# The last head of a gated-linear layer in a streaming encoder: its jobs over 21 slots for 18, its silu and splits at other places

## The reference

```python
b = jnp.cumsum(logf, axis=1)
inter = jnp.einsum('blhk,bhkv->blhv', qf * jnp.exp(b), s0)
decay = jnp.exp(jnp.where(causal, b[:, :, None] - b[:, None, :], -jnp.inf))
attn = jnp.einsum('blhk,bmhk,blmhk->bhlm', qf, kf, decay)
intra = jnp.einsum('bhlm,bmhv->blhv', attn, vf)
s_new = jnp.exp(b_last)[..., None] * s0 + jnp.einsum('blhk,blhv->bhkv', k_dec, vf)
...
o = o * lax.rsqrt(jnp.mean(o * o, axis=-1, keepdims=True) + EPS)
o = (o * g_onorm * jax.nn.silu(r)) @ w_out
```

## Time and profile before

| | us |
|---|---|
| median of 3 runs | 2671.1 (2668.15 to 2671.66) |
| the profiled execution | 2670.47 |
| its span, first to last instruction | 2668.7 |
| TensorE busy | 2531.0 |
| VectorE busy | 967.9 |
| ScalarE busy | 822.0 |
| GpSimd busy | 445.0 |
| mean granted TensorE clock, 1 is 2.4 GHz | 0.971 |

### The profile page before, as it was taken

The page is one execution under the profiler, slowest core; times in us unless marked ns, Lnnn a source line. Parts: engine busy times, 40 slices in busy tenths (PEclk is TensorE's granted clock), DMA queues, the critical chain, the costliest instruction groups (busy, mean ns, idle before and its releaser), DMA issues.

```text
span 2668.7 us, 41573 instructions
## 1 busy us (share of the span) xinstructions
PE 2531.0 (95%) x17454; PEld 2388.1 (89%) x17454; DVE 967.9 (36%) x1913; ACT 822.0 (31%) x1618; POOL 445.0 (17%) x186
## 2 busy tenths in 40 slices
PE   6999999898999999999998999889899999999997
PEld 5778878698999999999997977688899999999996
DVE  6354454416422222222228344425522222222227
ACT  4445444335311211120224355535411211211221
POOL 1101110111112211212211010112112212211210
PEclk9999999899999999999999999999999999999998
DMA  3101010013211111111113200103311111111113
GB/s 106 41 9 47 25 39 26 29 48 114 80 40 48 44 42 47 39 47 39 57 42 119 80 25 18 37 25 98 95 48 40 47 39 47 42 44 47 39 60 123
DMA packets 63088, 139.05 MB, mean 52 GB/s; under 512 B 8688, under 2 KB 39920, under 8 KB 62960
## 3 DMA queue, kind: packets, MB, share of 16 engines
q1 hardware_dynamic: 33984, 103.60, 12.0%
q10 hardware_dynamic: 28976, 33.64, 4.1%
HBM read 117.81 MB, written 19.40 MB: 51 GB/s over the span
## 4 chain that ended last, share of the span: by engine, by line
PE 77%; DVE 5%; issue 2%; ACT 2%; ACTq 0%; DMA 0%; DVEq 0%; SPq 0%
PE banks L201 51%; PE banks L181 19%; PE banks L1769 1%; DVE h_lo L548 1%; DVE norm_acc_x L477 1%; DVE norm_acc L463 1%; DVE y L524 1%; PE banks L1269 1%; PE banks L1288 1%; PE banks L323 0%; PE banks L1256 0%; PE banks L1296 0%; PE banks L1922 0%; PE banks L1925 0%; ACT y L1422 0%
## 5 line engine op out<-in xcount | busy, mean ns | idle before, releaser
L158 POOL TENSOR_TENSOR w_lo<-w_raw,w_hi 128x1024 fp32r<-128x1024 f32 x180 | 443.4, 2467 | 2151.3 <-ACT w_hi L151 2151.3
L181 PE MATMUL banks<-h_hi,w_hi 128*128 128x384 f32 (+1 forms) x1224 | 437.9, 358 | 8.1 <-POOL w_lo L158 5.3
L181 PE MATMUL banks<-h_lo,w_hi 128*128 128x384 f32 (+1 forms) x1224 | 415.9, 340 | 0.0
L181 PE MATMUL banks<-h_hi,w_lo 128*128 128x384 f32 (+1 forms) x1224 | 414.5, 339 | 0.0
L151 ACT CAST w_hi<-w_raw 128x1024 fp32r<-128x1024 f32 x180 | 187.0, 1047 | 468.0 <-DMA w_raw<-in_units 467.1
L201 PE MATMUL banks<-h_hi,w_hi 128*128 128x384 f32 (+1 forms) x1368 | 301.7, 329 | 0.0
L201 PE MATMUL banks<-h_hi,w_lo 128*128 128x384 f32 (+1 forms) x1368 | 301.3, 328 | 0.0
L201 PE MATMUL banks<-h_lo,w_hi 128*128 128x384 f32 (+1 forms) x1368 | 301.3, 328 | 0.0
L201 PE MATMUL banks<-mlp_a_hi,w_hi 128*128 128x384 f32 (+1 forms) x1344 | 296.6, 329 | 1.5 <-issue 1.3
L201 PE MATMUL banks<-mlp_a_lo,w_hi 128*128 128x384 f32 (+1 forms) x1344 | 295.1, 327 | 0.0
L201 PE MATMUL banks<-mlp_a_hi,w_lo 128*128 128x384 f32 (+1 forms) x1344 | 295.0, 327 | 0.0
(11 more groups left out here) (191 smaller groups left out, 3108.3 us busy)
## 6 DMA issues: line engine op xcount, KB each, us to landing
w_raw<-in_units SPq DMA_DIRECT2D x180, 512.0 KB, 3.5
x_scratch<-y ACTq DMA_DIRECT2D x48, 192.0 KB, 2.5
norm_x<-x_scratch ACTq DMA_DIRECT2D x48, 192.0 KB, 3.3
x_scratch<-y ACTq DMA_DIRECT2D x24, 160.0 KB, 1.8
norm_x<-x_scratch ACTq DMA_DIRECT2D x24, 160.0 KB, 3.1
y<-in_x SPq DMA_DIRECT2D x16, 192.0 KB, 4.7
norm_x<-in_x ACTq DMA_DIRECT2D x16, 192.0 KB, 3.5
out_y<-y SPq DMA_DIRECT2D x16, 192.0 KB, 2.7
```

The costliest lines, as they stand in the source:

```text
L158: c.nc.gpsimd.tensor_tensor(c.w_lo[:, s], c.w_raw[:, s], c.w_hi[:, s].bitcast(F32), ALU.subtract).then_inc(self.ready, 1)
L181: mm = chip.nc.tensor.matmul(out, w, x, start=(first and n == 0), stop=(last and n == 2))
```

## The change

Only `Gla` is touched. The probability rows of the windowed attention, kept without gaps between the two chunks of a pair (`ROW = WIN + 1`, `prob_keys`), are the same in both kernels.

- Head 3's jobs are spread over 21 slots, so over pairs 0 to 6, for 18 (pairs 0 to 5).
- Its weight casts move to later slots: unit 5 of the head from slot 6 to 8, 6 from 11 to 13, 7 from 13 to 15, 8 from 16 to 18, and 9 from 21 to 24.
- No end part stands in the loop any more; all four follow behind it.
- On ScalarE `silu(3)` and `early_high(0)` move from the end of pair 6 to the middle of pair 7, behind the copy of the turned keys and before the copy of the output. `early_high(1)` moves from the end of pair 7 to the same place in pair 8.
- On VectorE `early_low(0)` moves from the end of pair 6 to the end of pair 7, `early_low(1)` from the end of pair 7 to behind the inverse root of the outputs, and `early_low(2)` from there to behind the gating of block 1 and the first `low_parts`.
- At the start of head 0 the cast of unit 4 moves ahead of the first exponentials, and that of unit 5 ahead of the copy of the last v tile.

```diff
--- before.py
+++ after.py
@@ -1591,11 +1591,10 @@
     SCAN = 9 * CHUNK
     EARLY = 2 * (GH - 1)
     LEAD = 3 * KT * BMAX
-    STEPS = (PARTS * NPAIR, PARTS * NPAIR, PARTS * NPAIR, 18)
+    STEPS = (PARTS * NPAIR, PARTS * NPAIR, PARTS * NPAIR, 21)
     GATE_AT = (1, 3, 3)
     HIGHS = ({2: 6, 4: 7, 10: 8, 15: 9}, {4: 4, 6: 5, 10: 6, 13: 7, 16: 8, 19: 9}, {4: 4, 6: 5, 10: 6, 13: 7, 16: 8, 19: 9},
-             {4: 4, 6: 5, 11: 6, 13: 7, 16: 8, 21: 9})
-    FILL_AT = (23, 25)
+             {4: 4, 8: 5, 13: 6, 15: 7, 18: 8, 24: 9})
 
     def __init__(self, chip, name, before, after, ins):
         self.chip, self.before, self.after, self.ins = chip, before, after, ins
@@ -1844,8 +1843,6 @@
         def fill(h, slot):
             for job, k in self.plan[h][slot]:
                 job_step(job, k)
-            if h == GH - 1 and slot in self.FILL_AT:
-                end_early(self.FILL_AT.index(slot))
 
         def end_early(m):
 
@@ -1959,7 +1956,7 @@
                 output(h, p)
                 fill(h, self.PARTS * p + 2)
 
-        for m in range(len(self.FILL_AT), JOB_BANKS):
+        for m in range(JOB_BANKS):
             end_early(m)
         for i in range(2 * NB):
             if i == 0:
@@ -2189,12 +2186,12 @@
         take_start(2, 1)
         take_start(2, 2)
         chunk_decays(0)
+        ws.high(act, 4)
         level_exp(0)
         copy_value(7)
         level_exp(1)
-        ws.high(act, 4)
+        ws.high(act, 5)
         copy_value(8)
-        ws.high(act, 5)
         take_jobs(0, -1)
 
         for h in range(GH):
@@ -2211,6 +2208,11 @@
                 else:
                     take_jobs(h, slot)
                     level_exp(g + 2)
+                if h == GH - 1 and p == 7:
+                    silu(h)
+                    early_high(0)
+                if h == GH - 1 and p == 8:
+                    early_high(1)
                 if slot in self.HIGHS[h]:
                     ws.high(act, self.unit(h, self.HIGHS[h][slot]))
                 if h < GH - 1 and p == self.GATE_AT[h] + 1:
@@ -2233,11 +2235,6 @@
                     load_gain(h)
                 if h < GH - 2 and p == 6:
                     load_gate(h + 2)
-                if h == GH - 1 and p == 6:
-                    silu(h)
-                    early_high(0)
-                if h == GH - 1 and p == 7:
-                    early_high(1)
         output_root(GH)
         for j in range(NB):
             scale_outputs(GH, j)
@@ -2448,16 +2445,18 @@
                     gate_flat(h + 1)
                 if h < GH - 1 and p == self.GATE_AT[h] + 1:
                     gate_sums(h + 1)
-                if h == GH - 1 and p in (6, 7):
-                    early_low(p - 6)
+                if h == GH - 1 and p == 7:
+                    early_low(0)
         output_variance(GH)
         output_inverse(GH)
-        early_low(2)
+        early_low(1)
         for j in range(NB):
             gated(GH - 1, 2 * j)
             gated(GH - 1, 2 * j + 1)
             if j:
                 low_parts(j - 1)
+            if j == 1:
+                early_low(2)
         low_parts(NB - 1)
         self.vector_end_wave(dve)
```

## The result

The changed kernel takes 2649.61 us (median of 4 runs, 2646.81 to 2655.24) against 2671.38 (4 runs, 2668.15 to 2675.23): a ratio of 0.9921, 95% interval 0.9899 to 0.9942. The profiled execution took 2646.81 us, 23.7 less than that of before (2670.47).

A forecast was written before the change was run, and what follows sets the result against it. TensorE, busy 95% of the span, was taken as the bound. Start -0.3 us and head 3 with its tail -13.2 us sum to -13.5 us against the profiled execution's 2670.5 us: 2657.0 us, range 2651.5 to 2663.

The forecast's parts named there:

- Head 3: The last head of the gated-linear stage, through its tail: the stage ends at 537.7 us against 550.9, -13.2 us.
- The stall of pair 2: Head 3, pair 2: gating behind the update delays the state, a new TensorE stall of 2.2 us before the output's second half.
- rival C: Head 3, pairs 3 to 6: TensorE stays at 1.2 GHz, about 6.2 us per pair, 2682 us with all four; chance 0.04.
- Pair 7: Head 3, pair 7: ScalarE becomes the end, 6.95 us from scores to scores against 18.2.
- End parts: Four end parts behind head 3's loop: 72 matmuls, 12.7 us at full clock, 14.5 us with 1.8 for low clock.
- the late load: Weight load for the cast at slot 24: its 4.5 us wait is covered by the end parts and costs nothing.
- Rival D: Head 3, pairs 7 and 8 last 8.9 and 4.1 us, held by another round: 2 us more, 2659 us; chance 0.13.
- rival B: Low clock in head 3's pair 2 and end parts worth less, 2654.5 us, or more, 2659 us; chance 0.22.
- part 3: The tail, from head 3's turns to the stage's end, with the third low split moved: 4.2 us against 7.3.
- Part 4: Start of head 0, earlier weight cast: -0.3 us, with VectorE's differences blocked by GpSimd's split.
- rival A: Start of head 0: no lock on VectorE's differences, so the earlier cast gives 2.3 us, 2655.0 us; chance 0.12.
- none of these: Whole kernel: an outcome that neither the forecast nor any listed rival describes; chance 0.03.

The follow-up runs named there:

- gate_late: The changed kernel with VectorE gating turn jobs 4 and 5 of head 3 behind the state update of pair 2: 2644.74 us, 0.9904.
- head_only: The changed kernel with the start of head 0 put back to the old order: 2657.46 us, 0.9940 of the kernel before.
- pad_22: The changed kernel with 22 useless transpositions ahead of the scores of pair 1 of head 0: 2653.31 us, 0.9925 of the kernel before.
- silu_old: The changed kernel with the silu and the splits of blocks 0 and 1 back at the ends of pairs 6 and 7: 2659.53 us, 0.9950.
- tail_old: The changed kernel with VectorE's low split of block 2 back ahead of the gating: 2650.65 us, 0.9916 of the kernel before.
- before_pad24: The kernel before with 24 useless transpositions ahead of the scores of pair 1 of head 0: 2665.0 us against 2670.65, 0.9979.
- after_pad62: The changed kernel with 62 useless transpositions ahead of the scores of pair 1 of head 0: 2658.69 us, 0.9949 of the kernel before.
- copy_first: The changed kernel with the copy of the last v tile ahead of the second cast at the start of head 0: 2653.42 us, 0.9935.
- start_only: The kernel before with only the two weight casts moved at the start of head 0: 2665.27 us against 2672.67, 0.9972.
- slots18: The changed kernel with head 3's jobs over 18 slots again and its casts at the old slots but the last: 2655.21 us, 0.9932.
- after_again: The changed kernel without an edit, run a second time: 2649.57 us, 0.9915 of the kernel before.

## Why the prediction was right in head 3 and wrong in the time

**Head 3: -13.2 forecast, -12.6 measured.** The same code of head 3 lasts 113.5 to 117.0 us in the three traces that have the old one, and 102.6 to 105.2 in the six that have the new one unedited, by how much low clock falls into it: so a gain of some 11 us is sure (the means are 115.5 and 104.1), and that forecast and trace agree to 0.6 us is in part luck. Term by term, forecast and then after:
- First scores to the scores of pair 7: 74.5 us, measured 75.5 (424.40 to 499.87). The stall of pair 2 was forecast at 2.2 us and measures 1.87, and gate_late shows its cause. The pair itself was put at 11.7 us, with 0.7 beside it for the clock, and lasts 13.37: the clock stayed low for 3.4 us behind the stall, all of it paid and not half. This too depends on the execution: in head_only and pad_22 the same stall of 1.9 us leaves the clock at 1.00, and the pair lasts the 11.7 us. Pairs 3 to 6 keep the clock at 1.00, so rival C fell.
- Pair 7: 6.95, measured 6.87. silu_old shows that the order of the silu and the splits is the cause of 7.3 of the 11.4 us; the rest most likely goes with the end part that stood in this pair.
- Pair 8 to the first end part: 4.1, measured 3.74. End parts: 14.5, measured 14.89, with the late load covered as forecast. Rival D fell. Of rival B the costlier half came true in part: pair 2 pays in full, and low clock holds 6.8 us from 508.3 on, 4.6 of them under the end parts. Together that is 1.4 us over the forecast and not 2.
- Tail: 4.2, measured 3.84. But I put 3.1 us down to part 3, and tail_old gives back 0.5 of them. The rest most likely came with the end parts that stand together behind the loop, under which ScalarE and VectorE catch up; no run tests that alone.

**Part 4, a term mis-sized: -0.3 forecast, -2.6 measured** (2.26 of wait and 0.36 in the next pair; the 2.9 of the two profiles has some difference between executions in it). The wait is the 2.3 us of rival A, though A's reason, no exclusion, isn't what the trace shows. I took the case in which GpSimd's split blocks VectorE's differences, and bounded it by a scan of 3.4 us. VectorE and then GpSimd at this place in after:

```profile
95.79 1.09 DVE L2349 TENSOR_TENSOR gla_e<-gla_b 128x128 f32<-128x128 f32 x5
...
97.81 2.50 DVE L2369 TENSOR_TENSOR gla_qd<-gla_e,y 128x768 f32<-128x768 f32 x1 [0.53 <-ACT gla_e L2135]
```

```profile
95.61 3.88 POOL L158 TENSOR_TENSOR w_lo<-w_raw,w_hi 128x1024 fp32r<-128x1024 f32 x1 [52.94 <-ACT w_hi L151]
...
125.44 2.38 POOL L158 TENSOR_TENSOR w_lo<-w_raw,w_hi 128x1024 fp32r<-128x1024 f32 x1 [6.50 <-ACT w_hi L151]
```

Five differences take 1.09 us, as elsewhere. The split took 3.88 us for 2.38: it was the one held off, and by its length it got through when the train of 14 short differences was over (97.28 + 2.38 = 99.66, and it ended at 99.49). Then VectorE's multiply, which takes 0.89 us elsewhere (its next, at 107.74), took 2.50: it ended at 100.31, 0.82 us behind the split. The engines did exclude each other, as the earlier trace rows showed, but who paid was decided by when a short instruction stands in the way of a long one. The Trainium skill's rule (SBUF — State Buffer, "SBUF: two separate sides") is that whichever starts first has the port for the whole instruction; the trace agrees for the multiply. The split's row starts under two differences that run from 95.38 to 95.86; by the rule it waits for these; that the seven behind it would go first as well is not in it, and they did.

**The step that failed: heads 1 and 2, whose code is the same, are left out of the sum, that is, put at nothing.** The prediction has only that an earlier start carries over ("Behind the stage TensorE is the bound, so its start carries over"). It did carry over; but 6.1 us more came in heads 1 and 2, because two sparse stretches that drop the clock in before don't in after. That a shift alone can do this is shown by before_pad24 (more work, 5.6 us faster), and after_pad62 and copy_first have both stretches back. No rival had it; it falls under "none of these", 0.03. Had I looked for low clock in the unchanged heads, I would have found the row at 232 and put a range of 0 to 6 us on each shift upstream of it. With the part 4 that was measured, 2657.0 becomes 2654.7, and less the 6.1 it is 2648.6, beside 2646.8 in the profiled execution.

**What stays open.** The place of the sparse stretch counted from the start of the span doesn't tell low from not low: the copy of pair 2 in head 1 starts at 225.82 us in start_only (low) and 225.97 in slots18 (not low), at 228.99 in head_only (low) and 229.22 in before_pad24 (not low). Counted from the end of the low stretch near 106 us it does, in thirteen traces, but with one trace a kernel and 0.04 us at the border that is a reading and not a test. How often the changed kernel misses both drops isn't known: two traces of it do, but one of its four runs and one of the five of after_again took 2655.2 and 2656.3 us, 4 to 9 us more than the others, and have no trace. The 2.0 us behind the stage weren't followed up.

## What to carry to other kernels

A change to one stage moves everything behind it, and where a stretch behind it is sparse enough to drop the clock now and then, the shift alone is worth 3 us or more either way. So list the low-clock stretches of the whole span first, widen the range by those downstream of the edit, and judge an edit by the marks within its own stage beside the total. In an ordered list, look at what stands ahead of the instruction that others wait for: moving the silu and the splits behind the turned keys gave 10 us, moving two gatings behind the state 3.8 in head 3 (of 104.3), with no work taken out by either.

## What was not expected of the hardware

- The same code at the same busy time ran with a granted clock of 0.83 or 1.00 over 20 us, 3.05 us apart, with a shift of 1 to 3 us ahead of it, and for the changed kernel's order from one execution to another. 0.9 us of useless matmuls made a kernel 5.6 us faster.
- Only a short dip went before the fall of the clock at 232 us in before: TensorE idle for 0.91 us, and busy for 1.09 of 2 us. The same dip in after went without a fall.
- A train of short VectorE instructions held a GpSimd split off (3.88 us for 2.38), where a long scan had been the one to wait.
